# Where VectorE adds the halves of a finished mixing within its attention step

## The chip, the cores and the metric

The kernel runs on one core of a Trainium2 chip. Five engines work from queues of their own, each strictly in its program's order, and meet only through semaphores: TensorE (PE, with its weight loads shown as PEld), VectorE (DVE), ScalarE (ACT), GpSimd (POOL) and SyncE (SP, which issues the DMAs). The metric is the device time of one execution in microseconds (us); less is better.

## The reference

One inference step of a small diffusion backbone: two layers over 1024 latent tokens and 128 prompt tokens, width 1024. Each layer normalises and modulates the rows, projects them once (`w_in`), and runs three branches on the result: Fourier mixing, pooling, and attention with low-rank keys and values. The branches are gated, projected and added, and an output projection with a residual closes the layer. What matters here is the attention of a layer:

```
q = (rmsnorm(q_lat) @ w_q_up)          # 8 heads, 64 + 32 rotary columns
s = einsum('bqhd,bkhd->bhqk', q, k) * scale
p = softmax(s)                         # row maximum, exp, row sum
o = einsum('bhqk,bkhd->bqhd', p, v)    # "mixing" of the values
yc = (o * silu(c_z)) @ w_br_c
```

Latent queries see 1024 latent and 128 cached keys; the 128 prompt queries see 128 keys.

## The kernel before, in words

**Tiles and steps.** Queries are cut into 9 tiles of 128 rows in each head (8 latent, numbered 0 to 7, and the prompt tile, 8), so a layer has `TILES` = 72 tiles. The attention is one software pipeline of `STEPS` = 75 steps (0 to 74). Every engine runs its own loop over these steps, written out in its own block, and the order inside a step is a tuple of pairs: `PE_STEP` (L196) for TensorE, `DVE_STEP` (L198) for VectorE. Below, "position" is a step's number within its head, 0 to 8 (`h, j = divmod(s, TT)`).

**What a step does.** In step s TensorE turns (transposes) the probabilities of tile s-1 in three parts (`turn`, L1813), computes the three score parts of tile s+1 (`scores`, L1796), and multiplies turned probabilities with values (`mix`, L1824). ScalarE writes the high part of each turned piece to SBUF (`turned_high`, L850), and takes the exponentials of tile s (L834). VectorE writes the low part of each turned piece (`turned_low`, L1480: PSUM minus high part), the row sum and its inverse (`sum_inverses`, L1486 and L1491), the partial maxima of the next tile (`maxes`, L1467) and their minimum (`negmaxes`, L1473). Products run in three passes over a high and a low part of each operand (lines 1625 to 1627), which is why low parts exist.

**The mixing and its one bank.** A mixing covers two latent tiles (or the prompt tile): group 0 to 3, and 4 for the prompt. A group of two tiles is accumulated over 9 key blocks in five pieces: blocks 0-1 and 2-4 at mix slots 1 and 2 of one step, blocks 5, 6-7 and 8 at slots 0, 1, 2 of the next (`mix_slots`, L204). All mixings of the kernel use one PSUM bank, number 5 (`add(l, "mixed", 5, 1, ...)` in `bank_plan`). The product holds the high half of the values on 64 partitions and the low half on the other 64, so the two halves must be added: ScalarE lifts one half to SBUF (`lift`, L869, into `mixed_out`), VectorE adds the other half from PSUM (`unmix`, L1501), and frees the bank. GpSimd then multiplies the gates by it (`gated`, L1112). The next mixing starts in the very step in which the halves are added, at TensorE's mix slot 1, and `pe_takes(pe, l, "mixed", G)` in `mix` makes its first matmul wait for the bank that L1501 frees.

**Where the adding stands.** `mixed_in(s-1)` names the mixing that ended in the step before. It exists for positions 0, 2, 3, 5 and 7. In each of these steps VectorE does: the last maximum and `negmaxes`, a query product if there is one (`beside`, L1443, at positions 2 to 5), `unmix`, and then low part 0, row sum, maximum 0, low part 1, maximum 1, low part 2. ScalarE does `lift` first in its step and the high part 0 right behind it.

**Beside.** In positions 1 to 6 TensorE ends its step with a query or key product for the next head. In the steps past tile 71 it runs 16 matmuls of the gate projection (`gate_high`, L1860) at the place where the next mixing would begin.

Of the kernel before, what the change touches and what calls it, by code (L numbers as in the profile page):

```python
# [186 lines left out]
def score_item(m, c):  # L187
# [7 lines left out]
STEPS = TILES + 3  # L195
PE_STEP = (("turn", 0), ("score", 0), ("mix", 0), ("turn", 1), ("score", 1), ("mix", 1),  # L196
           ("turn", 2), ("score", 2), ("mix", 2))
DVE_STEP = (("beside", 0), ("unmix", 0), ("low", 0), ("sum", 0), ("max", 0), ("low", 1),  # L198
            ("max", 1), ("low", 2))
GATE_STEPS = (TILES - TT + 2, TILES - TT + 4)  # L200
BESIDE_STEPS = (1, 2, 3, 4, 5, 6)
# [64 lines left out]
def hybrid_step(nc, x_prompt, x_sample, cache_ckv, cache_krope, c, c_ctx, norm_g, w_mod, b_mod, w_in,  # L266
# [927 lines left out]
    def _(dve):  # L1194
# [87 lines left out]
        for l in range(DEPTH):  # L1282
# [186 lines left out]
            def negmaxes(m):  # L1469
                dve.wait_ge(S("partmax"), l * HEADS * (3 * TT - 2) + score_item(m, parts(m) - 1) + 1)  # L1470
                if m >= 2:
                    read_out(dve, l, "score", score_item(m - 2, parts(m - 2) - 1))
                v.tensor_reduce(negmax[:, m % 2:m % 2 + 1], partmax[:, m % 2, 0:parts(m)], AX.X, ALU.max, negate=True)\  # L1473
                    .then_inc(S("negmax"), 1)
# [31 lines left out]
            for s in range(STEPS):  # L1506
                if s < TILES:
                    maxes(s, parts(s) - 1)
                    negmaxes(s)
                for what, c in DVE_STEP:  # L1510
                    if what == "sum" and 1 <= s <= TILES:
# [461 lines left out]
```

## Time and profile before

| | us |
|---|---|
| median of 3 runs | 2216.41 |
| lowest, highest | 2216.18, 2216.81 |
| profiled execution | 2216.42 |
| its span, first to last instruction | 2214.3 |
| PE busy in the span | 2133.8 |
| DVE busy in the span | 1074.1 |
| ACT busy in the span | 887.3 |

The profile comes from one execution. The attention's first maximum (L1467) starts at 302.5 us of the span and the last add of layer 1 (L1501) at 1708.7 us; the stretches from 320 to 610 us and from 1414 to 1690 us lie wholly inside the attention of layer 0 and of layer 1, and in them three engines are loaded at once. A row of the timeline gives the start, the duration, the engine, the line, what is written from what, and in brackets the idle time ahead of the instruction and who ended it; where there are no brackets, the profile names no wait. Durations of neighbouring instructions on one engine overlap, since one starts before the one ahead has drained, so the distance from start to start is what an instruction takes of the engine.

### The profile page before, as it was taken

What the parts mean: (1) busy time and instruction counts of PE and PEld (TensorE: products, weight loads), DVE (VectorE), ACT (ScalarE), POOL (GpSimd) and SP (SyncE); (2) the same over time, 40 slices, a digit from 0 to 9 for tenths busy, and PEclk for the clock granted to TensorE, in tenths of its full rate; (3) what the DMA queues carried; (4) which work ended last, traced back from release to release, by engine and by line L of the source; (5) the groups of instructions that cost most, each with busy time, mean ns of one, the idle gap of its engine ahead of it and who ended that gap; (6) DMA issues with size and microseconds to landing.
All of it is one profiled execution on the core that took longest, in us unless ns stands there. A gap on an engine that the chain in (4) does not pass through costs nothing.

```text
span 2214.3 us, 36107 instructions
## 1 busy us (share of the span) xinstructions
PE 2133.8 (96%) x13185; PEld 2033.8 (92%) x13185; DVE 1074.1 (49%) x2775; ACT 887.3 (40%) x2223; POOL 732.0 (33%) x656
## 2 busy tenths in 40 slices
PE   6999999999999999999999999999999999999997
PEld 4899888888899999999989998888888999999997
DVE  2441268888764668663162314888886111120213
ACT  2421267787831212113152214787787122111312
POOL 1323133443422234333441312343443123433242
PEclk9999999999999999999999999999999999999999
DMA  9811000000353333324255100000014111111232
GB/s 280 266 30 31 26 1 1 2 1 2 121 156 86 93 84 101 81 64 144 73 194 163 40 1 25 2 1 1 2 35 171 48 37 48 43 46 39 63 124 86
DMA packets 194622, 155.68 MB, mean 70 GB/s; under 512 B 8636, under 2 KB 186000, under 8 KB 193424
## 3 DMA queue, kind: packets, MB, share of 16 engines
q1 hardware_dynamic: 194448, 153.38, 22.6%
q8 instruction: 106, 1.74, 0.3%
q14 instruction: 68, 0.56, 0.1%
HBM read 124.89 MB, written 28.48 MB: 69 GB/s over the span
## 4 chain that ended last, share of the span: by engine, by line
PE 85%; DVE 6%; ACT 4%; issue 3%; DMA 1%; POOL 0%; SPq 0%; DVEq 0%; POOLq 0%; ACTq 0%
PE ps L1625 24%; PE ps L1627 23%; PE ps L1626 23%; PE ps L1817 5%; PE ps L1842 3%; PE ps L1843 2%; DVE partmax L1467 1%; DVE probsT L1480 1%; ACT probs L834 1%; PE ps L1635 1%; ACT probsT L850 1%; DMA raw<-in_w_mod 1%; PE ps L1860 1%; DVE xn_high L1226 1%; PE ps L1821 1%
## 5 line engine op out<-in xcount | busy, mean ns | idle before, releaser
L1625 PE MATMUL ps<-xn_high,split_br 128*128 128x384 f32 x1584 | 531.7, 336 | 0.0
L1627 PE MATMUL ps<-xn_high,split_br 128*128 128x384 f32 x1584 | 529.4, 334 | 0.0
L1626 PE MATMUL ps<-xn_low,split_br 128*128 128x384 f32 x1584 | 529.3, 334 | 0.0
L967 ACT ACTIVATE sigmoids<-ps 128x384 f32<-128x384 f32 x144 | 70.4, 492 | 613.1 <-PE ps L1627 613.1
L1009 POOL TENSOR_TENSOR split_br<-raw,split_br 128x1024 fp32r<-128x1024 f32 x82 | 198.0, 2416 | 320.4 <-ACT split_br L695 320.4
L1626 PEld LDWEIGHTS ps<-xn_low,split_br 128*128 128x128 f32 x1584 | 297.5, 188 | 0.0
L1625 PEld LDWEIGHTS ps<-xn_high,split_br 128*128 128x128 f32 x1584 | 297.4, 188 | 0.0
L1627 PEld LDWEIGHTS ps<-xn_high,split_br 128*128 128x128 f32 x1584 | 297.4, 188 | 0.0
L1480 DVE TENSOR_TENSOR probsT<-ps,probsT 128x384 fp32r<-128x384 f32 x384 | 213.3, 556 | 74.9 <-ACT sum_inv_rows L857 36.4
L834 ACT ACTIVATE probs<-ps,negmax 128x384 f32<-128x384 f32 (+1 forms) x400 | 229.7, 575 | 38.2 <-DVE negmax L1473 37.6
L850 ACT ACTIVATE probsT<-ps 128x384 fp32r<-128x384 f32 x384 | 188.8, 492 | 67.7 <-PE ps L1817 40.3
L1467 DVE TENSOR_REDUCE partmax<-ps 128x1 f32<-128x384 f32 (+1 forms) x400 | 212.1, 534 | 2.0 <-PE ps L1627 1.8
L1817 PE MATMUL ps<-ident,probs 128*128 128x128 f32 x1168 | 197.4, 276 | 7.6 <-DVE probsT L1480 3.7
L1161 POOL TENSOR_TENSOR merged<-merged,products 128x384 f32<-128x384 f32 x90 | 92.3, 1026 | 334.7 <-DVE products L1559 333.9
L1559 DVE TENSOR_TENSOR products<-ps,sigmoids 128x384 f32<-128x384 f32 x96 | 53.5, 557 | 292.8 <-PE ps L1627 240.2
L1625 PE MATMUL ps<-split_br,xn_high 128*128 128x256 f32 (+1 forms) x576 | 182.0, 316 | 5.3 <-DVE xn_low L1229 5.1
L1627 PE MATMUL ps<-split_br,xn_low 128*128 128x256 f32 (+1 forms) x576 | 178.7, 310 | 0.0
L1626 PE MATMUL ps<-split_br,xn_high 128*128 128x256 f32 (+1 forms) x576 | 178.7, 310 | 0.0
L1625 PE MATMUL ps<-kT,qT 128*128 128x384 f32 (+1 forms) x400 | 163.1, 408 | 12.1 <-issue 10.5
L1817 PEld LDWEIGHTS ps<-ident,probs 128*128 128x128 f32 x1168 | 132.0, 140 | 46.1 <-issue 39.9
L1842 PE MATMUL ps<-probsT,head_values 128*128 128x256 f32 x576 | 156.1, 291 | 16.5 <-DVE mixed_out L1501 16.5
L1843 PE MATMUL ps<-probsT,head_values 128*128 128x256 f32 x576 | 150.3, 281 | 0.0
(228 smaller groups left out, 4156.8 us busy)
## 6 DMA issues: line engine op xcount, KB each, us to landing
raw<-in_w_in SPq DMA_DIRECT2D x74, 512.0 KB, 4.0
raw<-in_w_mod SPq DMA_DIRECT2D x48, 512.0 KB, 5.3
park_high<-xn_high SPq DMA_DIRECT2D x6, 1536.0 KB, 6.2
park_low<-xn_low SPq DMA_DIRECT2D x6, 1536.0 KB, 10.6
xn_high<-park_high SPq DMA_DIRECT2D x2, 4608.0 KB, 15.9
rows<-in_x_sample SPq DMA_DIRECT2D x16, 512.0 KB, 6.9
raw<-in_w_out SPq DMA_DIRECT2D x16, 512.0 KB, 6.6
rows_mid<-rows SPq DMA_DIRECT2D x9, 512.0 KB, 2.6
```

The lines of the kernel that those rows point to most:

```text
L834: a.activation((P0, P1)[m % 2][:, c * CH:c * CH + w], PS[:, b, 0:w], ACT.Exp, bias=negmax[:, m % 2:m % 2 + 1], accum_out=partsum[:, m % 2, ...
L850: ins = a.activation(turned_place(m, gg, 0), PS[:, b, 0:n * P].rearrange("p (k c) -> p k c", k=n), ACT.Copy)
L1009: g.tensor_tensor(d[:, 1], raw_unit(n), d[:, 0].bitcast(F32), ALU.subtract).then_inc(S("split_low"), 1)
L1161: g.tensor_tensor(Y[:, u % KF, sl], Y[:, u % KF, sl], prod[:, q % 2, :], ALU.add).then_inc(S("y_sum"), 1)
L1467: v.tensor_reduce(partmax[:, m % 2, c:c + 1], PS[:, b, 0:w], AX.X, ALU.max).then_inc(S("partmax"), 1)
L1480: v.tensor_tensor(turned_place(m, gg, 1), PS[:, b, 0:n * P].rearrange("p (k c) -> p k c", k=n), turned_place(m, gg, 0).bitcast(F32), ALU.s ...
L1625: mm(out, wh, xh, start=first, stop=False)
L1626: mm(out, wh, xl, start=False, stop=False)
L1627: return mm(out, wl, xh, start=False, stop=last)
L1817: ins = nc.tensor.transpose(PS[:, b, q * P:(q + 1) * P], (P0, P1)[m % 2][:, (3 * gg + q) * P:(3 * gg + q + 1) * P], ident[:])
L1842: mm(PS[:, b, 0:w], vhl, xh, start=(kt == 0 or gr == 4), stop=False)
L1843: ins = mm(PS[:, b, 0:w], vhl, xl, start=False, stop=last)
```

## The change

One pair of `DVE_STEP` moves: `("unmix", 0)` from the second to the fifth place.

```diff
-DVE_STEP = (("beside", 0), ("unmix", 0), ("low", 0), ("sum", 0), ("max", 0), ("low", 1),
+DVE_STEP = (("beside", 0), ("low", 0), ("sum", 0), ("max", 0), ("unmix", 0), ("low", 1),
             ("max", 1), ("low", 2))
```

No instruction is added or taken away, on any engine; TensorE's, ScalarE's and GpSimd's order stays. Three places show it.

VectorE, position 5 of a head, layer 0, before. `mixed_out` is the add, `probsT` a low part, `partmax` a maximum; `lifted` is ScalarE's lift, `pt_high` its high part, `bank_full5` the finished mixing.

```order
L1473 TENSOR_REDUCE negmax<-partmax 128x1 [waits bank_free1,partmax]
L1501 TENSOR_TENSOR mixed_out<-ps,mixed_out 64x256 [waits lifted,bank_full5]
L1480 TENSOR_TENSOR probsT<-ps,probsT 128x3x128 [waits pt_high,bank_full6]
L1486 TENSOR_REDUCE rowsum<-partsum 128x1 [waits bank_free4]
L1491 RECIPROCAL sum_inv<-rowsum 128x1 [waits bank_full6,rowsum]
L1467 TENSOR_REDUCE partmax<-ps 128x1 [waits bank_full3]
L1480 TENSOR_TENSOR probsT<-ps,probsT 128x3x128 [waits pt_high,bank_full7]
```

The same place on VectorE now:

```order
L1473 TENSOR_REDUCE negmax<-partmax 128x1 [waits bank_free1,partmax]
L1480 TENSOR_TENSOR probsT<-ps,probsT 128x3x128 [waits pt_high,bank_full6]
L1486 TENSOR_REDUCE rowsum<-partsum 128x1 [waits bank_free4]
L1491 RECIPROCAL sum_inv<-rowsum 128x1 [waits bank_full6,rowsum]
L1467 TENSOR_REDUCE partmax<-ps 128x1 [waits bank_full3]
L1501 TENSOR_TENSOR mixed_out<-ps,mixed_out 64x256 [waits lifted,bank_full5]
L1480 TENSOR_TENSOR probsT<-ps,probsT 128x3x128 [waits pt_high,bank_full7]
```

Four instructions now stand ahead of the add. Positions 2 and 3 look the same; at position 7 the maximum is missing (the prompt tile comes next and has one score part), so three stand ahead.

VectorE, position 0 of a head, before; the tile turned there is the prompt tile, whose only low part comes at the place of low part 2:

```order
L1473 TENSOR_REDUCE negmax<-partmax 128x1 [waits bank_free3,partmax]
L1501 TENSOR_TENSOR mixed_out<-ps,mixed_out 64x256 [waits lifted,bank_full5]
L1486 TENSOR_REDUCE rowsum<-partsum 128x1 [waits bank_free4]
L1491 RECIPROCAL sum_inv<-rowsum 128x1 [waits bank_full6,rowsum]
L1467 TENSOR_REDUCE partmax<-ps 128x1 [waits bank_full3]
L1467 TENSOR_REDUCE partmax<-ps 128x1 [waits bank_full4]
```

The same place on VectorE now:

```order
L1473 TENSOR_REDUCE negmax<-partmax 128x1 [waits bank_free3,partmax]
L1486 TENSOR_REDUCE rowsum<-partsum 128x1 [waits bank_free4]
L1491 RECIPROCAL sum_inv<-rowsum 128x1 [waits bank_full6,rowsum]
L1467 TENSOR_REDUCE partmax<-ps 128x1 [waits bank_full3]
L1501 TENSOR_TENSOR mixed_out<-ps,mixed_out 64x256 [waits lifted,bank_full5]
L1467 TENSOR_REDUCE partmax<-ps 128x1 [waits bank_full4]
```

Here the sums and one maximum have moved ahead of the add, and no low part.

TensorE at position 5, the same in both kernels: turn 0, scores 0, turn 1, scores 1, and the next mixing's first matmul, which waits for `bank_free5`, the semaphore that the add raises:

```order
L1817 MATMUL ps<-ident,probs_95 128x128 [waits bank_free6,bank_free2]
L1817 MATMUL ps<-ident,probs_95 128x128 x2
L1625 MATMUL ps<-kT,qT 128x384 [waits bank_free3,q_low]
L1626 MATMUL ps<-kT,qT 128x384
L1627 MATMUL ps<-kT,qT 128x384
L1817 MATMUL ps<-ident,probs_95 128x128 [waits bank_free7,bank_free3]
L1817 MATMUL ps<-ident,probs_95 128x128 x2
L1625 MATMUL ps<-kT,qT 128x384 [waits bank_free4]
L1626 MATMUL ps<-kT,qT 128x384
L1627 MATMUL ps<-kT,qT 128x384
L1842 MATMUL ps<-probsT,head_values 128x256 [waits bank_free6,bank_free5]
```

Nothing of TensorE's order moved; turn 2, scores 2 and the rest of the mixing are queued behind that last row.

## Rows read from the trace of the kernel before

**Rows 1.** The page, busy time of each engine, share of the span, instructions.
```profile
PE 2133.8 (96%) x13185; PEld 2033.8 (92%) x13185; DVE 1074.1 (49%) x2775; ACT 887.3 (40%) x2223; POOL 732.0 (33%) x656
```

**Rows 2.** Windows: us, busy PE, PEld, DVE, ACT, POOL; granted clock, DMA share, GB/s.
```profile
40.00:60.00 20.00, 11.97 (x79) 9.38 (x77) 14.72 (x27) 11.40 (x19) 9.05 (x6) 0.65 0.95 315
320.00:610.00 290.00, 273.62 (x1858) 247.11 (x1857) 236.40 (x676) 231.75 (x697) 117.38 (x142) 1.00 0.07 24
1414.00:1690.00 276.00, 259.34 (x1761) 234.55 (x1761) 225.29 (x646) 218.99 (x659) 110.63 (x134) 1.00 0.07 25
```

**Rows 3.** Waits, whole span: engine, line <- waited for: us, times, longest.
```profile
DVE mixed_out L1501 <- ACT mixed_out L869: 33.7, 42, 4.1
PEld ps L1842 <- DVE mixed_out L1501: 26.4, 36, 1.0
PE ps L1842 <- DVE mixed_out L1501: 16.5, 34, 0.7
```

**Rows 4.** Waits of PE from 320 to 610 us.
```profile
PE ps L1842 <- DVE mixed_out L1501: 7.8, 16, 0.7
```

**Rows 5.** Timeline, position 5 of a head.
```profile
445.52 0.49 ACT L850 ACTIVATE probsT<-ps 128x384 fp32r<-128x384 f32 x1
445.60 0.43 DVE L1501 TENSOR_TENSOR mixed_out<-ps,mixed_out 64x256 f32<-64x256 f32 x1 [0.58 <-ACT mixed_out L869]
446.12 0.56 DVE L1480 TENSOR_TENSOR probsT<-ps,probsT 128x384 fp32r<-128x384 f32 x1
446.24 0.29 PE L1842 MATMUL ps<-probsT,head_values 128*128 128x256 f32 x1
446.77 0.16 DVE L1491 RECIPROCAL sum_inv<-rowsum 128x1 f32<-128x1 f32 x1
446.85 0.54 DVE L1467 TENSOR_REDUCE partmax<-ps 128x1 f32<-128x384 f32 x1
447.31 0.55 DVE L1480 TENSOR_TENSOR probsT<-ps,probsT 128x384 fp32r<-128x384 f32 x1
```

**Rows 6.** Timeline, position 7.
```profile
454.61 0.43 DVE L1501 TENSOR_TENSOR mixed_out<-ps,mixed_out 64x256 f32<-64x256 f32 x1 [0.59 <-ACT mixed_out L869]
455.09 0.38 PE L1842 MATMUL ps<-probsT,head_values 128*128 128x256 f32 x1 [0.32 <-DVE mixed_out L1501]
455.77 0.16 DVE L1491 RECIPROCAL sum_inv<-rowsum 128x1 f32<-128x1 f32 x1
```

**Rows 7.** Timeline, position 0.
```profile
463.43 0.43 DVE L1501 TENSOR_TENSOR mixed_out<-ps,mixed_out 64x256 f32<-64x256 f32 x1
463.89 0.15 DVE L1486 TENSOR_REDUCE rowsum<-partsum 128x1 f32<-128x1 f32 x1
463.91 0.39 PE L1842 MATMUL ps<-probsT,head_values 128*128 128x256 f32 x1 [0.72 <-DVE mixed_out L1501]
464.27 0.56 DVE L1467 TENSOR_REDUCE partmax<-ps 128x1 f32<-128x384 f32 x1
```

**Rows 8.** Timeline, position 2, in one head and in the head before it.
```profile
391.58 0.56 DVE L1480 TENSOR_TENSOR probsT<-ps,probsT 128x384 fp32r<-128x384 f32 x1
391.80 0.22 PE L1842 MATMUL ps<-probsT_prompt,head_values 128*128 128x128 f32 x1
...
431.27 0.41 DVE L1501 TENSOR_TENSOR mixed_out<-ps,mixed_out 64x256 f32<-64x256 f32 x1
431.60 0.56 DVE L1480 TENSOR_TENSOR probsT<-ps,probsT 128x384 fp32r<-128x384 f32 x1
432.37 0.23 PE L1842 MATMUL ps<-probsT_prompt,head_values 128*128 128x128 f32 x1
```

**Rows 9.** Timeline, position 3.
```profile
435.68 0.27 DVE L1501 TENSOR_TENSOR mixed_out<-ps,mixed_out 64x128 f32<-64x128 f32 x1
435.92 0.56 DVE L1480 TENSOR_TENSOR probsT<-ps,probsT 128x384 fp32r<-128x384 f32 x1
436.79 0.28 PE L1842 MATMUL ps<-probsT,head_values 128*128 128x256 f32 x1
```

## The prediction, made before the changed kernel ran

> **What bounds the kernel now.** I read the page first: PE is busy 2133.8 of 2214.3 us [rows 1], so on the whole the kernel is as long as TensorE's queue, and a change on VectorE can only move the time through what TensorE waits for. The change touches the attention alone, so the windows inside it come next: of 290 us in layer 0 PE is busy 273.6, DVE 236.4 and ACT 231.8, and of 276 us in layer 1 259.3, 225.3 and 219.0 [rows 2]. PE leads there too, with 16.4 us idle per 290, while the other two have some 20% of air. Then I read who is waited for. The add L1501 is on TensorE's path already: the first matmul of a mixing waited for it 34 times (16.5 us), and its weight load 36 times (26.4 us) [rows 3]; the load runs ahead of the matmul, so the second sum is not wholly lost time. In the layer 0 window 7.8 of the 16.4 idle us are that wait [rows 4]. Last comes the timeline, one step for each position at which an add stands [rows 5 to 9]. The adds have no slack to give: the largest distance from an add's end to the matmul that needs its bank is 436.79 - 435.95 = 0.84 us [rows 9], in positions 0 and 7 the matmul starts 0.05 us after the add ends [rows 6, 7], and at position 5 it is 446.24 against 446.03 [rows 5].
>
> **What moves.** In each step with an add, low part 0, the row sum, its inverse and maximum 0 go ahead of it. Nothing is added or removed, so DVE has the same work. What changes is when bank 5 is free, and behind the waiting matmul stand turn 2, scores 2, the rest of the mixing and the beside products: all that TensorE does next, and through it ScalarE's high part 2, VectorE's low part 2, and the next step.
>
> The one open question is when low part 0 can start once the add is out of its way. It needs ScalarE's high part 0, which ScalarE writes behind the lift. At position 5 that ends at 445.52 + 0.49 = 446.01 and low part 0 starts at 446.12 [rows 5]. The add sat in a hole that VectorE had anyway. So I let low part 0 start where it starts now, and put the add after maximum 0. The distance from low part 0 to the slot behind maximum 0 is 447.31 - 446.12 = 1.19 us [rows 5]. To this comes the add itself and 0.05 us to the matmul [rows 6].
>
> **The five positions**, each as the new start of the mixing's first matmul less the old one:
>
> - Position 5 [rows 5]: 447.31 + 0.43 + 0.05 = 447.79, against 446.24: 1.55 us.
> - Position 7 [rows 6]: no maximum there. The slot behind the inverse is 0.08 us after its start (446.77 to 446.85 in [rows 5]), so 455.77 + 0.08 + 0.43 + 0.05 = 456.33, against 455.09: 1.24 us.
> - Position 0 [rows 7]: no low part 0. The row sum takes the add's slot at 463.43, the maximum follows 464.27 - 463.89 = 0.38 later, the add 0.46 after that (446.85 to 447.31), so 464.27 + 0.48 = 464.75, against 463.91: 0.84 us.
> - Position 2 [rows 8]: in one head low part 0 is at 431.60, so 431.60 + 1.19 + 0.41 + 0.05 = 433.25, against 432.37: 0.88 us. In the head before, 391.58 + 1.19 + 0.43 + 0.05 = 393.25, against 391.80: 1.45 us. I take the first for three heads and the second for four.
> - Position 3 [rows 9]: 435.92 + 1.19 + 0.27 + 0.05 = 437.43, against 436.79: 0.64 us.
>
> Counts per layer: positions 5 and 7 in all eight heads, positions 0, 2 and 3 in seven (the add closes the head before). The adds past tile 71 lie beside `gate_high` and cost nothing. Sum: 8 x 1.55 + 8 x 1.24 + 7 x 0.84 + 3 x 0.88 + 4 x 1.45 + 7 x 0.64 = 12.4 + 9.9 + 5.9 + 2.6 + 5.8 + 4.5 = 41.1 us per layer.
>
> **What is given back, and what comes on top.** While TensorE stands, the others catch up, so idle time that it had elsewhere in the step can vanish. At most that is the idle time which is not this wait, 16.4 - 7.8 = 8.6 us per layer [rows 2, 4]; at least it is nothing. Most of it stands in front of turns and scores held by work that itself follows TensorE's pace, so I take 2.5. On top, a mixing's first matmul behind a wait shows 0.38 us where one that didn't wait shows 0.29 [rows 5, 6]: 0.1 us for each of the 22 starts per layer at positions 5, 2 and 3 (8 + 7 + 7) that don't wait now, 2.2 in all. Net 41.1 - 2.5 + 2.2 = 40.8 us per layer, 81.6 us in both.
>
> GpSimd's gate product waits for the add and now starts later, by the same 1 to 2 us. What waits for GpSimd here is the next lift, which at its nearest is a whole step away (add at position 2, lift at position 3; the two adds stand 435.68 - 431.27 = 4.4 us apart [rows 8, 9]), and the step gets longer too: nothing for it.
>
> The sum belongs to the profiled execution: 2216.42 us, of which 2214.3 are span and 2.1 lie around it; it agrees with the median of 2216.41. 2216.4 + 81.6 = 2298.
>
> In half of the heads the add is followed by its neighbour only when it has ended (463.43 to 463.89, 0.46 us), in the others sooner (431.27 to 431.60, 0.33 us) [rows 7, 8]. The Trainium skill has a rule for it (VectorE: DVE Perf Modes, section "Two Vector instructions with no wait between them"): an instruction whose operands start in another quadrant of 32 partitions than those of the one before is held until VectorE is empty. The add of an odd head works on partitions 64 to 127, everything around it starts at 0, and the rows agree. By that rule the moved add is held behind the maximum as well, about 0.1 us in half of the 74 places, and the sum would be 4 us larger, 2302; I leave it out of the sum and let the upper end cover it.
>
> **Rivals.**
>
> 1. *Positions 7 and 0 are absorbed.* Around 454 to 464 us TensorE waits more than elsewhere (0.32 and 0.72 us in one head [rows 6, 7]), so ScalarE and VectorE may set the pace there and a late mixing be hidden. Then their 15.8 us per layer drop out: 2 x (41.1 - 15.8 - 2.5 + 2.2) = 50, so 2266. Against it: what TensorE does behind the mixing is turn 2 of the same tile, which high part 2 and low part 2 need, so the engines that would hide the stall are fed by it.
> 2. *The other side: faster.* VectorE waits 33.7 us in 42 places for the lift right ahead of the add [rows 3]. If that wait were the price of the old order, low part 0, sums and maximum would fill it, and all of it would come back: 2216 - 34 = 2183. For this low part 0 must be ready before the lift is done, and the new end of the add must still come ahead of the matmul. It decides at a slack of about 1.7 us (1.19 + 0.43 + 0.05), and the largest in the rows is 0.84. ScalarE writes the high part behind the lift, so the hole is not usable either.
> 3. *No difference.* The same hole serves and TensorE's stalls are all made up by its idle time: 8.6 us per layer can't cover 41.1. It would need slips in several positions at once.
> 4. *The clock falls.* The granted clock is 1.00 in both attention stretches and 0.65 between 40 and 60 us, where PE is busy 12.0 of 20 [rows 2]: the upper level of 2.4 GHz throughout, and a mix of it with the lower one of 1.2. Idle gaps of 0.7 us [rows 7] left it at the upper level. If gaps of about 2 us brought its mean to 0.9 in the attention, 533 us of matmuls would grow by some 53 us on top: 2351. The Trainium skill warns of this (TensorE: Matmul & The Clock Gate, section "HAM oscillation"): a TensorE that keeps waiting between bursts of matmuls falls back to the low clock each time. Its example has DMA waits longer than its bursts, while here some 4 us of matmuls would stand between two waits; no row here shows gaps of 2 us in such a load.
>
> **Chances.** My forecast 0.82, rival 1 or something between it and the forecast 0.11, rival 2 0.02, rival 3 0.02, rival 4 0.03. The forecast's own range: with all of the idle time given back, 2 x (41.1 - 8.6) = 65 us, 2281; with nothing given back, the restart, the held adds, and position 2 and 3 of each layer's last head as dear as position 5, some 2 x (41.1 + 2.2 + 2 + 1) = 93 us, 2309. The range given takes in most of rival 1 and a little above: 2268 to 2313. What a measurement of this kernel can tell from no change is about 0.2%, 4.4 us. Faster by more than that is rival 2, 0.02; within it rival 3, 0.02; slower the rest, 0.96.
>
> **What the profile after would show.** Right: DVE's order in the waits turns round, low part 0 waits for ACT's high part (about 1 us at positions 5 and 7), and L1501 has no wait of its own; the first mixing matmul waits at all five positions, about 74 times, some 80 to 120 us in sum instead of 16.5; from low part 0 to the add 1.2 us; DVE, ACT and PE busy times as before within a few us; the time before 320 us and after the attention of each layer unchanged in length. Wrong: waits of L1842 that are short because low part 0 starts earlier than its high part allowed before; waits as long as said, but PE's other idle time shrunk by more than 17 us (rival 1); a granted clock under 1.00 in the attention (rival 4). If the wait for L1501 grows and the span doesn't, TensorE was not the bound.

## The result, and the profile after

The changed kernel takes 2302.6 us (median of 4 runs, 2301.8 to 2305.2), the kernel before in the same comparison 2216.6 (2216.2 to 2216.9): a ratio of 1.039 [1.0372, 1.0408], so 86.0 us slower. The forecast was 2298, and 2302 by the rule of the held add. One of the executions of experiment 5 fell into the chip's slow state (2647 us at a mean granted clock of 0.75) and is left out of every number here. The profiled execution took 2302.7 us, of which 2300.6 are span: 86.3 more than before.

The page of the changed kernel first: busy time of each engine, share of the span, instructions.

```profile
PE 2147.9 (93%) x13185; PEld 2046.7 (89%) x13185; DVE 1073.4 (47%) x2775; ACT 890.4 (39%) x2223; POOL 731.3 (32%) x656
```

Against [rows 1] no engine has more instructions, and the 14 us more of PE are far less than 86 (matmuls restart behind a wait, and the clock falls at times, see below; I didn't measure the two apart). The rest is idle time, and the waits of the changed kernel (whole span) name it:

```profile
PEld ps L1842 <- DVE mixed_out L1501: 117.6, 74, 2.8
PE ps L1842 <- DVE mixed_out L1501: 95.3, 74, 2.5
...
DVE mixed_out L1501 <- ACT mixed_out L869: 13.0, 4, 4.1
```

All 74 adds that have a mixing behind them now hold TensorE up; before it was 34 for the matmul and 36 for its load [rows 3]. The matmul's waits grew by 78.8 us. VectorE's own wait for the lift went from 42 places to 4, and that bought nothing.

Next the windows. The attention is longer, so each stretch is lengthened from [rows 2]; the first holds nearly as many matmuls as before (1826 where it was 1858), the second more (1825 where it was 1761), and only the first is compared (columns as in [rows 2]):

```profile
320.00:646.00 326.00, 274.38 (x1826) 246.46 (x1824) 233.02 (x667) 230.88 (x688) 113.31 (x139) 0.98 0.06 22
...
1443.00:1769.00 326.00, 274.10 (x1825) 246.15 (x1824) 233.22 (x668) 231.03 (x688) 113.27 (x139) 0.98 0.06 22
```

PE was idle 16.4 us of 290 before and is idle 51.6 of 326 now. Of these 51.6, 43.7 are the wait for the add:

```profile
PE ps L1842 <- DVE mixed_out L1501: 43.7, 35, 2.1
```

The timeline of the changed kernel, at the positions of [rows 5 to 9] in their order (5; 7; 0; 2 in one head and in the next; 3):

```profile
462.69 0.56 DVE L1480 TENSOR_TENSOR probsT<-ps,probsT 128x384 fp32r<-128x384 f32 x1 [1.09 <-ACT probsT L850]
463.43 0.54 DVE L1467 TENSOR_REDUCE partmax<-ps 128x1 f32<-128x384 f32 x1
464.00 0.43 DVE L1501 TENSOR_TENSOR mixed_out<-ps,mixed_out 64x256 f32<-64x256 f32 x1
464.48 0.39 PE L1842 MATMUL ps<-probsT,head_values 128*128 128x256 f32 x1 [1.49 <-DVE mixed_out L1501]
...
473.32 0.56 DVE L1480 TENSOR_TENSOR probsT<-ps,probsT 128x384 fp32r<-128x384 f32 x1 [1.10 <-ACT probsT L850]
473.98 0.17 DVE L1491 RECIPROCAL sum_inv<-rowsum 128x1 f32<-128x1 f32 x1
474.18 0.43 DVE L1501 TENSOR_TENSOR mixed_out<-ps,mixed_out 64x256 f32<-64x256 f32 x1
474.66 0.39 PE L1842 MATMUL ps<-probsT,head_values 128*128 128x256 f32 x1 [1.69 <-DVE mixed_out L1501]
...
483.71 0.43 DVE L1501 TENSOR_TENSOR mixed_out<-ps,mixed_out 64x256 f32<-64x256 f32 x1
484.20 0.39 PE L1842 MATMUL ps<-probsT,head_values 128*128 128x256 f32 x1 [1.42 <-DVE mixed_out L1501]
...
401.77 0.54 DVE L1467 TENSOR_REDUCE partmax<-ps 128x1 f32<-128x384 f32 x1
402.34 0.43 DVE L1501 TENSOR_TENSOR mixed_out<-ps,mixed_out 64x256 f32<-64x256 f32 x1
402.82 0.33 PE L1842 MATMUL ps<-probsT_prompt,head_values 128*128 128x128 f32 x1 [1.40 <-DVE mixed_out L1501]
...
447.25 0.54 DVE L1467 TENSOR_REDUCE partmax<-ps 128x1 f32<-128x384 f32 x1
447.71 0.41 DVE L1501 TENSOR_TENSOR mixed_out<-ps,mixed_out 64x256 f32<-64x256 f32 x1
...
452.91 0.27 DVE L1501 TENSOR_TENSOR mixed_out<-ps,mixed_out 64x128 f32<-64x128 f32 x1
453.24 0.39 PE L1842 MATMUL ps<-probsT,head_values 128*128 128x256 f32 x1 [0.49 <-DVE mixed_out L1501]
```

Two things are to be seen. Low part 0 now has the 1.1 us wait for ScalarE's high part that the forecast gave it, and the add has none. And each first matmul starts 0.05 or 0.06 us after its add has ended.

The length of a step is the distance between successive starts of the minimum (L1473). In the third and the fourth head of layer 0 it is, in us:

| position | before | after | forecast of the growth | measured growth |
|---|---|---|---|---|
| 0 | 3.01 / 2.88 | 3.72 / 3.59 | 0.84 | 0.71 |
| 2 | 5.00 / 4.44 | 6.02 / 5.32 | 1.45 / 0.88 | 1.02 / 0.88 |
| 3 | 4.60 / 4.59 | 5.49 / 5.34 | 0.64 | 0.89 / 0.75 |
| 5 | 4.43 / 4.43 | 5.94 / 6.07 | 1.55 | 1.51 / 1.64 |
| 7 | 6.10 / 6.12 | 7.33 / 7.48 | 1.24 | 1.23 / 1.36 |
| 1, 4, 6, 8 together | 17.55 / 17.57 | 17.68 / 17.57 | 0 | 0.13 / 0.00 |

The positions without an add keep their length, within 0.6 us per layer. Nothing is made up later.

### The profile page after: what moved, and what is told of

It reads as the page before. It is cut to its first block, busy times and chain, and to the rows that moved or that the text cites. A ratio compares the mean times of both kernels' runs of the same rounds, so it can differ in the third digit from the quotient of the medians.

```text
span 2300.6 us, 36107 instructions
## 1 busy us (share of the span) xinstructions
PE 2147.9 (93%) x13185; PEld 2046.7 (89%) x13185; DVE 1073.4 (47%) x2775; ACT 890.4 (39%) x2223; POOL 731.3 (32%) x656
## 4 chain that ended last, share of the span: by engine, by line
PE 82%; DVE 8%; issue 4%; ACT 4%; DMA 1%; POOL 1%; SPq 0%; DVEq 0%; ACTq 0%; POOLq 0%
PE ps L1625 22%; PE ps L1627 22%; PE ps L1626 22%; PE ps L1817 5%; PE ps L1842 3%; PE ps L1843 3%; DVE partmax L1467 2%; ACT probsT L850 1%; DVE mixed_out L1501 1%; DVE probsT L1480 1%; DMA raw<-in_w_mod 1%; PE ps L1635 1%; PE ps L1860 1%; ACT mixed_out L869 1%; PE ps L1821 1%
## 5 line engine op out<-in xcount | busy, mean ns | idle before, releaser
L1842 PE MATMUL ps<-probsT,head_values 128*128 128x256 f32 x576 | 163.9, 303 | 79.9 <-DVE mixed_out L1501 79.9
L1842 PEld LDWEIGHTS ps<-probsT,head_values 128*128 128x128 f32 x576 | 112.3, 195 | 97.7 <-DVE mixed_out L1501 97.7
L1817 PEld LDWEIGHTS ps<-ident,probs 128*128 128x128 f32 x1168 | 137.0, 143 | 37.0 <-issue 32.6
```

What stands on the lines that cost most here:

```text
L1817: ins = nc.tensor.transpose(PS[:, b, q * P:(q + 1) * P], (P0, P1)[m % 2][:, (3 * gg + q) * P:(3 * gg + q + 1) * P], ident[:])
L1842: mm(PS[:, b, 0:w], vhl, xh, start=(kt == 0 or gr == 4), stop=False)
```

## The experiments

Each comparison stands against the kernel before, timed on the same chip in the same series: 2217.0 for experiments 1 to 4, 2216.7 for 5 to 8, 2216.8 for 9 to 12.

### 1 to 3: the late order at some positions only

The theory: each position pays for itself, by TensorE's wait for bank 5. The rival: the positions share a stall, so that one alone costs less or more than its part of the sum.

```diff
+LATE_AT = (7, 0)                # experiment 2: (5,)   experiment 3: (2, 3)
-                for what, c in DVE_STEP:
+                for what, c in (DVE_LATE if s % TT in LATE_AT else DVE_STEP):
```

`DVE_LATE` is the changed order, `DVE_STEP` stays the old one.

> The add stands behind maximum 0 at positions 7 and 0 of each head only, and where it was before at positions 2, 3 and 5. Theory (every late add stalls TensorE by what the rows give, and nothing hides it): 2 x (8 x 1.24 + 7 x 0.84) = 31.6 us, with the held adds of odd heads some 33: 2248 to 2250. Rival (ScalarE and VectorE set the pace around positions 7 and 0, because the next head's weights are cut on VectorE there): nothing or a few us, 2217 to 2222. If the stretches at 1.2 GHz of the changed kernel come from TensorE's waits at position 7, they are seen here too; if they come from the load of all five waits in a head, they aren't.

> The add stands behind maximum 0 at position 5 alone. Theory: 2 x 8 x (1.55 + 0.1 for the restart) = 26 us, less up to 0.1 us a place given back: 2241 to 2243. Rival (the wait here fills idle time that TensorE has later in the step and the head): under 13 us, below 2230.

> The add stands behind maximum 0 at positions 2 and 3 alone. Theory: 2 x (3 x 0.88 + 4 x 1.45 + 7 x 0.64) = 25.8 us, plus 2.8 for restarts, less some 4 for idle time of TensorE at these positions: 2239 to 2243. The three parts (positions 7 and 0, 5, 2 and 3) then add up to the 86 us of the whole change. Rival (the parts overlap, for example because a late add at position 2 makes the lift at position 3 late as well): the three parts sum to 70 us or less, and this one is 10 to 15 us.

Measured: 2248.9 for positions 7 and 0 (1.0142 [1.0127, 1.0157], +31.9), 2243.3 for position 5 (1.0118 [1.0103, 1.0133], +26.3), 2244.0 for positions 2 and 3 (1.012 [1.0105, 1.0135], +26.9). Together that is 85.1, and the whole change costs 86.0. The first is inside its expectation, the other two lie 0.3 and 1.0 us above theirs (the four runs of experiment 3 spread from 2241.6 to 2246.7). The waits of the three kernels in this order:

```profile
PE ps L1844 <- DVE mixed_out L1503: 46.7, 34, 1.7
```

```profile
PE ps L1844 <- DVE mixed_out L1503: 40.0, 48, 2.5
```

```profile
PE ps L1844 <- DVE mixed_out L1503: 41.7, 60, 2.1
```

Less the 16.5 of [rows 3] these are 30.2, 23.5 and 25.2. In each kernel only the chosen positions have the changed kernel's step lengths (position 5: 5.94 / 6.06; position 2: 6.02 / 5.33), the others those of before, but for a few steps in a layer's last head where the clock fell (last section). The positions add up.

### 4: behind low part 0, ahead of the sums

```diff
-DVE_STEP = (("beside", 0), ("unmix", 0), ("low", 0), ("sum", 0), ("max", 0), ("low", 1),
+DVE_STEP = (("beside", 0), ("low", 0), ("unmix", 0), ("sum", 0), ("max", 0), ("low", 1),
```

> The add stands one place later than before, behind low part 0 and ahead of the row sum, in all positions. Theory (cost is the distance on VectorE from low part 0 to the add, 0.47 us instead of 1.19): position 5 446.12 + 0.47 + 0.48 - 446.24 = 0.83, position 7 0.98, position 0 nothing (no low part 0 there), position 2 0.16 and 0.73, position 3 nothing: 2 x (6.6 + 7.8 + 0.5 + 2.9) = 36 us and 2 to 3 for restarts: 2253 to 2256. Rival (low part 0's own wait for ScalarE's high part is the whole loss, and what follows it is hidden): the same as the full change, 2290 to 2303.

Measured: 2256.5, 1.0173 [1.0156, 1.019], +39.5, half a microsecond above the expectation. The waits:

```profile
PE ps L1841 <- DVE mixed_out L1500: 52.1, 56, 1.7
```

At position 0, which has no low part 0, the step is back at 3.00 us, and position 5 takes 5.21 / 5.36 instead of 5.94 / 6.07. So the 86 us follow how many instructions stand ahead of the add: 39.5 for the low part, 46.5 for the sums and the maximum.

### 5 and 6: a whole mixing at slot 2

To see whether the bank is the only price, the mixing's first piece is taken away from slot 1, so that its first matmul comes after turn 2 and scores 2. Experiment 5 does so on the changed kernel, experiment 6 on the kernel before.

```diff
-slots[1], slots[2] = (h, (j - 3) // 2, (0, 1)), (h, (j - 3) // 2, (2, 3, 4))
+slots[2] = (h, (j - 3) // 2, (0, 1, 2, 3, 4))
```

The pieces of group 3 and of the prompt tile move to slot 2 in the same way.

> The changed kernel, and TensorE starts each mixing at mix slot 2 (key blocks 0 to 4 in one go) instead of at slot 1, so that turn 2 and scores 2, some 1.3 us of matmuls, stand ahead of the wait. Theory (the whole loss is the wait of the mixing's first matmul): the waits shrink from about 1.4 to 0.1 us at positions 5, 7, 0 and go at most of 2 and 3, so most of the 86 us comes back: 2215 to 2235. Rival (the later low parts and maxima in VectorE's order carry the loss): 2290 to 2303.

> The kernel before with the same later start of a mixing. Theory: the waits of TensorE for the add at positions 7 and 0 go (0.32 and 0.6 to 0.7 us, 16.5 us in all), and what ScalarE and VectorE need there may take half of them: 2200 to 2212. Rival (the mixing then ends its first step later, in front of the next turn, and the query or key product with it): 2217 to 2225.

Measured: 2254.3 for the late order (1.0167 [1.015, 1.0184]) and 2230.3 for the early one (1.0058 [1.0043, 1.0073]). Both results lie outside the theory and outside the rival. The early order lost 13.6 us where a gain was expected, by its profile to turns that wait for low parts (first fence the kernel before, second experiment 6; the 30.4 us more, less the 16.5 of [rows 3] that are gone, fit the loss). And in the late order, where TensorE hardly waits for the add (third fence, experiment 5), 24.0 us against experiment 6 remained.

```profile
PE ps L1817 <- DVE probsT L1480: 3.7, 20, 0.3
```

```profile
PE ps L1817 <- DVE probsT L1480: 34.1, 56, 1.4
```

```profile
PEld ps L1842 <- DVE mixed_out L1501: 5.4, 22, 0.3
```

So there is a second path behind the add that isn't TensorE's bank. The next runs look for it.

### 7 and 8: two banks for the mixings

```diff
-add(l, "score", 0, 5, ...)
-add(l, "mixed", 5, 1, ...)
+add(l, "score", 0, 4, ...)
+add(l, "mixed", 4, 2, ...)
```

Experiment 7 is the changed kernel with this, experiment 8 the kernel before with it. The wait for the bank is gone in both, with TensorE's order untouched; the scores have a bank less.

> The changed kernel with two PSUM banks for the mixings (4 and 5), and four instead of five for the scores. Theory (one bank is what ties TensorE to the add): the next mixing doesn't wait for the add at all, so the order of VectorE costs next to nothing: within 10 us of the same kernel with the add in its old place, and 2205 to 2235. Rival (VectorE's order itself is the loss): 60 us or more above the same kernel with the old order.

> The kernel before with two PSUM banks for the mixings and four for the scores: the partner of the run above. Theory: the 16.5 us of TensorE's waits for the add are gone, and if four score banks are enough, 2200 to 2210. If four are too few, scores wait for exponentials and both kernels with two banks are slower than 2216 by the same amount.

Measured: 2298.3 (1.0372 [1.0355, 1.039]) and 2271.9 (1.0247 [1.0231, 1.0262]). Experiment 7 missed its theory and its rival. Experiment 8 went its second way, that four score banks are too few, but the two kernels aren't slower by the same amount. The new division of the banks costs 55.3 us, with what the second mixing bank saves already taken off; the waits of experiment 8 show scores that wait for ScalarE's exponentials to free a bank (1.0 us in 2 places in the kernel before):

```profile
PE ps L1625 <- ACT probs L834: 46.6, 55, 1.5
```

And the late order still costs 26.4 us, about as in 5 against 6, though not one wait for the add stands in front of TensorE. The step lengths place them. Position 7 takes 7.32 / 7.46 in experiment 7 and 6.08 / 6.10 in 8, 16.5 us over both layers; position 8 adds another 10.2, and the rest differs little. The part of position 8 is mostly the clock: in 8 of its 14 places the granted clock fell to the lower level right behind position 7, and there the step is 0.65 to 1.57 us longer than where it didn't (4.52 us in the first head, 3.26 in the second), 8.4 us in sum (last section). So some 18 of the 26.4 us are left for a second path. The timeline of experiment 7 at position 7:

```profile
469.06 0.73 POOL L1109 TENSOR_TENSOR branch<-sum_inv_rows,branch 64x256 f32<-64x256 f32 x1 [0.26 <-POOL kT L1096]
...
473.55 0.43 DVE L1501 TENSOR_TENSOR mixed_out<-ps,mixed_out 64x256 f32<-64x256 f32 x1
474.12 0.74 POOL L1112 TENSOR_TENSOR branch<-mixed_out,branch 64x256 f32<-64x256 f32 x1 [4.34 <-DVE mixed_out L1501]
474.90 0.28 ACT L857 ACTIVATE sum_inv_rows<-ps 128x128 f32<-128x128 f32 x1 [0.34 <-POOL branch L1112]
475.28 0.56 DVE L1480 TENSOR_TENSOR probsT<-ps,probsT 128x384 fp32r<-128x384 f32 x1 [0.71 <-ACT sum_inv_rows L857]
475.84 1.27 POOL L1096 TENSOR_TENSOR kT<-key_value,kT 64x512 fp32r<-64x512 f32 x1
475.92 1.46 DVE L1344 TENSOR_SCALAR wq_head<-wq_raw 128x16 fp32r<-128x16 f32 x4
```

and of experiment 8:

```profile
470.45 1.26 POOL L1096 TENSOR_TENSOR kT<-key_value,kT 64x512 fp32r<-64x512 f32 x1
...
471.76 0.39 DVE L1344 TENSOR_SCALAR wq_head<-wq_raw 128x16 fp32r<-128x16 f32 x4
```

Read from the add it is a chain round three engines: the add, GpSimd's gate product (L1112), ScalarE's copy of the row sums (L857, which waits for the gate product by `act.wait_ge(S("gated"), ...)` at L854, for an add of the same step at positions 5 and 7), VectorE's low part 2 behind that copy, and VectorE's next work. At its end there is a second price: the four small instructions that scale the next head's weights (L1344) take 1.46 us instead of 0.39, because they run beside GpSimd's product L1096, which in experiment 8 was over when they began. In experiment 5 they take 1.46 or 1.47 us as well, in all twelve heads that have them within the attention, and there the granted clock stayed at 1.00, so its 24.0 us are without the clock's part.

### 9: the key product ahead of the gate product

On experiment 7, GpSimd's order alone is changed, so that L1096 comes out of the way of L1344.

```diff
-                if group:
-                    gated(*group)
-                for kind, hh, i in beside(s):
-                    if kind == "q":
-                        q_low(hh, i)
-                    else:
-                        k_split(hh, i)
+                for kind, hh, i in beside(s):
+                    if kind == "k":
+                        k_split(hh, i)
+                if group:
+                    gated(*group)
+                for kind, hh, i in beside(s):
+                    if kind == "q":
+                        q_low(hh, i)
```

> The changed kernel with two mixing banks, and GpSimd splits the next head's key piece (L1094, L1096) ahead of its gate product (L1109, L1112) instead of behind it. With two banks the late add still cost 26 us, nearly all at position 7, where VectorE's four small weight instructions (L1344) took 1.46 us together instead of 0.39 while GpSimd's key split, pushed back by the late add, ran beside them. Theory (VectorE and GpSimd collide there): the key split is over before VectorE comes to the weights, L1344 is back at 0.16 us each, and the time falls by about 0.9 us x 12 heads = 11 us: 2286 to 2289. Rival (the low part 2 that waits for the sums and the gate product is all of it, and the slow L1344 is idle time shown as work): no change, 2296 to 2300.

Measured: 2282.0, 1.0292 [1.0276, 1.0307], 16.3 us less than experiment 7 (timed in another series, whose kernel before differs by 0.1 us) and more than the 9 to 12 expected. The source line's view (times, and the shortest, median and longest in ns) of the weight scaling, in experiment 7 and then in experiment 9:

```profile
L1344 DVE TENSOR_SCALAR wq_head<-wq_raw x64: 154/160/1235, 161.3 to 1688.6; 128x16 fp32r<-128x16 f32 x64
```

```profile
L1345 DVE TENSOR_SCALAR wq_head<-wq_raw x64: 154/160/163, 162.2 to 1680.9; 128x16 fp32r<-128x16 f32 x64
```

Position 7 falls to 6.56 / 6.57, 9.7 us over the twelve heads: that is the collision, near the 11 us of its theory. The rest isn't the collision. The falls of the clock at position 8 are gone too, some 8 us, while position 5 grew by 3.6 us, since the gate product now stands behind the key product and ScalarE's copy waits longer for it (experiment 7, then experiment 9):

```profile
ACT sum_inv_rows L857 <- POOL branch L1112: 4.4, 17, 0.3
```

```profile
ACT sum_inv_rows L857 <- POOL branch L1112: 17.8, 30, 1.1
```

What is left, 10.1 us against experiment 8, fits the chain through L857, and a part of it comes from this edit itself; I haven't taken that wait away by itself. It asks for more than the data do: the row sums that L857 overwrites are read by the product ahead, L1109, which in experiment 7 was over at 469.79, four microseconds ahead of the add, but L854 waits for L1112. A semaphore raised behind L1109 would open this chain; no run here shows what that gives.

### 10 to 12: the other direction

If the distance to the add is what TensorE pays, an earlier add should gain where TensorE waits before the change. Experiment 10, on the kernel before, puts the add ahead of the last maximum at position 0. Experiment 11 moves ScalarE's lift at positions 5 and 7 from the start of that step to the step before, ahead of the copy of the key product. Experiment 12 does both.

```diff
 # experiment 10, VectorE; the add in the loop over DVE_STEP is left to the other positions
+                if s and s % TT == 0:
+                    unmix(*mixed_in(s - 1))
                 if s < TILES:
                     maxes(s, parts(s) - 1)
 # experiment 11, ScalarE
-                if s and mixed_in(s - 1):
+                if s and mixed_in(s - 1) and (s - 1) % TT not in (4, 6):
                     lift(*mixed_in(s - 1))
...
+                if s % TT in (4, 6):
+                    lift(*mixed_in(s))
                 for it in beside(s):
                     if it[0] == "k":
```

> The kernel before, with the add at position 0 of each head moved the other way: ahead of the last maximum and negmax of the tile. Theory (TensorE's wait for the add is what counts): the wait there, 0.59 to 0.72 us, 14 times, goes: up to 9 us, 2207 to 2210. Rival (negmax comes 0.46 us later, and ScalarE, which waits 0.87 us for it there, sets the pace around the prompt tile): no gain or a loss of up to 6 us, 2216 to 2223.

> The kernel before, with ScalarE lifting the finished mixing ahead of the next head's key piece (L887) at positions 4 and 6 instead of behind it, so that the add of positions 5 and 7 can start some 0.6 us earlier, in a hole of VectorE. Theory: TensorE's wait at position 7 (0.32 us, 16 times) goes, and high part 0 comes no later: 5 us, 2210 to 2213. Rival (the wait moves to what ScalarE does behind the lift, since its own queue is as long as before): no change, 2215 to 2218.

> The two edits together on the kernel before: the add first at position 0, and the lift ahead of the key piece at positions 4 and 6. Theory: both waits are independent, 9 + 5 us: 2202 to 2206. Rival: whichever of the two gives nothing alone gives nothing here, 2207 to 2217.

Measured: 2218.0 for experiment 10, 1.0003 [0.9994, 1.0012], no difference, as its rival had it; 2208.0 for 11, 0.9959 [0.9944, 0.9973], 2 us better than its theory; 2208.4 for 12, 0.9957 [0.9942, 0.9972], as its rival had it. Experiment 10 took TensorE's wait away and gave it back at once; its waits:

```profile
ACT probs L834 <- DVE negmax L1473: 43.9, 29, 2.1
...
PE ps L1844 <- DVE mixed_out L1501: 7.5, 20, 0.6
```

The second sum was 16.5 [rows 3], the first 37.6 before: the maximum that the add overtook is what ScalarE waits for. The steps at position 0 shrank to 2.65 us and those at position 8 grew from 3.27 to 3.62 and 3.86. Experiment 11 beats both kernels, by 8.7 us against the one before. Its waits and its timeline at such a place:

```profile
DVE mixed_out L1503 <- ACT mixed_out L869: 15.9, 12, 4.1
...
PE ps L1844 <- DVE mixed_out L1503: 10.8, 18, 0.7
```

```profile
451.56 0.38 ACT L869 ACTIVATE mixed_out<-ps 64x256 f32<-64x256 f32 x1
451.96 0.59 ACT L887 ACTIVATE key_value<-ps 64x512 f32<-64x512 f32 x1
452.32 0.43 DVE L1503 TENSOR_TENSOR mixed_out<-ps,mixed_out 64x256 f32<-64x256 f32 x1
```

VectorE waits for the lift in 12 places instead of 42, and position 7 takes 5.46 / 5.56 instead of 6.10 / 6.12: 0.55 to 0.66 us less in twelve of the 16 heads and 0.36 in two, 7.9 us in sum, with another 1.7 at positions 5 and 8; 8.7 arrive in the time. The wait that the change under study filled was worth removing, only from ScalarE's side.

## Why the prediction was right

- **The add is on TensorE's path, without slack.** Right: 74 waits as said, 95.3 us in the range of 80 to 120, the matmul 0.05 us behind the add, and experiments 1 to 3 pay position by position.
- **Low part 0 can't start sooner.** Right: it waits 1.09 and 1.10 us for its high part at positions 5 and 7, and so the hole at the lift served nobody.
- **The five positions.** Right in sum, and in part by luck. Over all heads the steps grew by 41.7 us per layer (mean of both) where 41.1 was forecast: 12.4 at position 5 (forecast 12.4), 10.9 at position 7 (9.9), 4.9 at position 0 (5.9), 6.9 at position 2 (8.4), 6.2 at position 3 (4.5) and 0.5 at the others. So 2.5 us too many at two positions made up for 2.7 too few at two others. In single steps, position 2 in the dearer heads was set too high (1.45 against 1.02), position 3 too low (0.64 against 0.89 and 0.75). Experiment 3 has both positions late and doesn't tell the two apart.
- **Adds past tile 71, put at nothing.** Nearly: from the last minimum to the first product behind the attention it took 0.7 and 0.8 us longer.
- **Given back 2.5, on top 2.2 per layer.** The restart of the matmul is there (0.39 at position 5 where it was 0.29). Idle time elsewhere is 51.6 - 43.7 = 7.9 us in the first window against 8.6 before, in windows of not quite the same content, so at most some 0.7 per layer is given back and not 2.5: that term was too large.
- **The held add, left out of the sum.** It should have been in. The add of an odd head follows the start of the maximum by 463.43 to 464.00 = 0.57 us, that of an even one by 447.25 to 447.71 = 0.46; over the whole trace the distance is 0.56 to 0.58 us in 26 places and 0.45 or 0.46 in 32. The Trainium skill's rule (VectorE: DVE Perf Modes, section "Two Vector instructions with no wait between them") agrees with these rows. The price was a little under the forecast's 4 us: places with such an add grew by 0.13 or 0.14 us more than their neighbours at positions 5, 7 and 3, some 3 us in 22 places, but by the same 0.71 at position 0, where the old order held the add too (3.01 us against 2.88). That the sum with this term, 2302, is so near 2302.6 is luck, given the offsets above and the 2.5 us that weren't given back.
- **"GpSimd: nothing for it."** Wrong as a step, though it moved no number. Besides the next lift, ScalarE's copy of the row sums waits for the gate product, and that chain, with the collision at its end, keeps 24.0 us in experiment 5 and some 18 in experiment 7, where the clock adds 8. In the changed kernel it runs beside TensorE's stall and comes free. At position 7 the two paths are of nearly equal length (7.33 / 7.48 us in the changed kernel, 7.32 / 7.46 in experiment 7), and removing one leaves the other; at position 5 TensorE's is the longer one (5.94 against 5.33).
- **The rivals.** Absorbed positions (1): no, experiment 1 shows +31.9 for them, where the forecast had 2 x 15.8 = 31.6. Faster (2) and no difference (3): no. The clock (4): its sign came, a granted clock under 1.00 in the attention, but at a mean of 0.98 and for some 2.5 us. (Its price was worked out too low: at a mean of 0.9, 533 us of matmuls would grow by 533 / 0.9 - 533 = 59 us, not 53.)
- **The signs.** Besides, PE is busy 14 us longer where a few were said; the order of the waits, their number and their sum came as said.

## What to carry to other kernels

Where an accumulator has one bank, the engine that empties it sets when TensorE may go on: find the distance from the add's end to the waiting matmul first, and if it is 0.05 us, each instruction that is put ahead of the add is paid in full, whatever wait it fills on its own engine. Fill such a wait from the side of the engine that is waited for (here ScalarE's lift, 8.7 us gained), rather than by reordering the one that waits. And when a run that removes the named wait keeps part of the loss, look for a second chain from the same instruction, in the timelines of both orders side by side, and look at the granted clock of both before all of the rest is put down to the chain (8 of the 26 us here).

## What the runs showed of the hardware

**The clock.** The granted clock fell inside the attention of the changed kernel, which it never did in the kernel before ([rows 2] have 1.00 in both stretches): eight times, for some 3.4 us each, always right behind TensorE's wait for the add at position 7 (1.56 to 1.69 us). The dip at 566 us in windows (columns as in [rows 2]), and the window after another wait at position 7, without one:

```profile
565.00:566.00 1.00, 0.00 (x0) 0.00 (x0) 0.94 (x4) 1.00 (x5) 0.00 (x0) 1.00 0.03 8
566.00:570.00 4.00, 3.92 (x19) 3.92 (x20) 1.95 (x8) 1.58 (x7) 3.20 (x4) 0.57 0.00 0
...
476.00:480.00 4.00, 3.06 (x23) 2.80 (x21) 3.29 (x14) 1.74 (x6) 2.42 (x3) 1.00 0.02 6
```

TensorE stood still from 565 to 566 us, and then ran at the lower level (1.2 GHz) while the same 128x256 matmul took longer; the timeline in the dip and two heads before it:

```profile
568.05 0.41 PE L1842 MATMUL ps<-probsT,head_values 128*128 128x256 f32 x1
...
475.92 0.28 PE L1842 MATMUL ps<-probsT,head_values 128*128 128x256 f32 x1
```

A dip cost little here, because TensorE had idle time to lose behind it. Positions 7 and 8 together took 10.72 us in a head with one and 10.61 in a like head without, 10.96 against 10.74 in two others; in six places it was 0.04 to 0.29 us, and 0.6 and 0.8 in the last head of the two layers (5.12 and 5.33 us at position 7, where experiment 1 has 4.52 without a dip). That is some 2.5 us in all. The forecast's rival of a mean clock of 0.9 had 53; the mean in the attention was 0.98.

Experiment 1 was also meant to tell where the dips come from, and does: with positions 7 and 0 alone late the mean over the attention is 0.98 again, with position 5 alone or positions 2 and 3 alone the clock stays at 1.00 up to the last head of a layer. There it did fall in experiment 2 behind a wait of 2.47 us (position 5) and in experiment 3 behind one of 2.08 (position 3). The changed kernel has the same two waits in its last heads, and no dip behind them. So which wait is followed by a dip isn't settled by its length alone.

A dip isn't cheap everywhere. In experiment 7 TensorE stands still for 2.0 us at position 7 (not for the add), and in 8 of 14 places the clock fell behind that, into position 8, where TensorE then has no idle time:

```profile
341.04 0.41 PE L1625 MATMUL ps<-kT,qT 128*128 128x384 f32 x1 [2.00 <-issue]
```

```profile
342.00:346.00 4.00, 4.00 (x21) 4.00 (x20) 2.92 (x13) 1.42 (x5) 0.00 (x0) 0.59 0.00 0
```

These cost 0.65 to 1.57 us each. In experiment 5 the wait at this place is 1.39 us, in experiment 9 it is gone, and in neither did a dip follow there. The Trainium skill (TensorE: Matmul & The Clock Gate, section "HAM oscillation") tells of a kernel in which the clock falls after every wait for a DMA; here it came after some waits and not after others of the same length.

**VectorE and GpSimd.** A 128x16 instruction of 160 ns took 1235 ns beside a GpSimd product of 1.27 us (experiment 7), and 163 at most once that product was moved (experiment 9). The profile shows the blocked instruction as busy, not as waiting, so only its longest duration betrays it. The changed kernel has it in three of twelve heads, each time where the clock had fallen (0.94 or 0.95 us for the four instructions instead of 0.39). This agrees with the Trainium skill (SBUF - State Buffer, section "Who interferes with whom"), by which such a scaling can take both port pairs of VectorE, of which one is GpSimd's too, and whoever comes second is blocked until the first is done.
